# Seven block products on half tokens for the fourth group of the first feed-forward's second projection, beside the norms that follow it

## The reference, cut to what matters

```python
nm = rmsnorm(h, mlp_norm_g[l])
a = jnp.square(jax.nn.relu(jnp.einsum('bsd,df->bsf', nm, w_ff1[l])))    # 1024 -> 4096
h = h + jnp.einsum('bsf,fd->bsd', a, w_ff2[l])                          # 4096 -> 1024
...
x = rmsnorm(h, final_norm_g)                                            # end of layer one
...
xn = rms_norm(x, norm1_g)                                               # layer two
proj = xn @ w_in                                                        # q_sb first
```

## Time and profile before

| | us |
|---|---|
| median of 3 runs | 1363.39 (1362.97 to 1363.85) |
| the profiled execution, device time | 1364.07 |
| its span from first to last instruction | 1362.7 |
| PE busy | 1348.6 (99%) |
| DVE busy | 873.2 (64%) |
| ACT busy | 819.9 (60%) |
| POOL busy | 334.6 (25%) |

### The profile page before, as it was taken

One profiled execution on the slowest core, in us unless ns is written; L12 is line 12 of the kernel. 1 busy time (PEld: TensorE's weight loads), 2 busy tenths in 40 slices (PEclk: granted clock), 3 DMA queues, 4 the chain that ended last, 5 costly groups with the idle time before them and its releaser, 6 DMA issues.

```text
span 1362.7 us, 19539 instructions
## 1 busy us (share of the span) xinstructions
PE 1348.6 (99%) x7510; PEld 1135.7 (83%) x7510; DVE 873.2 (64%) x1548; ACT 819.9 (60%) x1235; POOL 334.6 (25%) x306
## 2 busy tenths in 40 slices
PE   9999999999999999999999999999999999999999
PEld 6977956789899898887777788888888898889889
DVE  6055466577576682357787779975437785568557
ACT  6575566753544545666577767775666645754553
POOL 0211101235343251111211121211113252315214
DMA  7976643925436137876654685668888536824733
GB/s 251 238 165 144 148 117 78 231 32 196 99 98 179 33 125 191 193 169 144 149 129 111 137 217 125 137 145 182 201 214 203 110 118 194 184 47 164 188 51 109
DMA packets 57969, 202.45 MB, mean 149 GB/s; under 512 B 6450, under 2 KB 7019, under 8 KB 57748
## 3 DMA queue, kind: packets, MB, share of 16 engines
q0 software_dynamic: 25632, 93.09, 36.4%
q1 hardware_dynamic: 31380, 106.24, 23.7%
q10 hardware_dynamic: 864, 1.87, 0.4%
HBM read 199.05 MB, written 2.12 MB: 148 GB/s over the span
## 4 chain that ended last, share of the span: by engine, by line
PE 77%; DVE 11%; ACT 8%; DMA 3%; issue 2%; SPq 0%; POOL 0%; DVEq 0%; ACTq 0%
PE bank L660 18%; PE bank L667 18%; PE bank L664 18%; PE bank L698 17%; DVE eb L1730 2%; PE bank L813 1%; ACT WL L1038 1%; ACT eb L1198 1%; ACT WH L1030 1%; ACT zs L1152 1%; PE bank L885 1%; DVE eb L1725 1%; DMA WL<-in_w_in 1%; DMA WL<-in_w_gu 1%; DMA RAW<-in_w_in 1%
## 5 line engine op out<-in xcount | busy, mean ns | idle before, releaser
L660 PE MATMUL bank<-NH,WH 128*128 128x512 f32 x1152 | 459.8, 400 | 0.3 <-ACT NH L1207 0.3
L664 PE MATMUL bank<-NL,WH 128*128 128x512 f32 x1152 | 448.1, 390 | 0.6 <-DVE NL L1470 0.5
L667 PE MATMUL bank<-NH,WL 128*128 128x512 f32 x1152 | 448.1, 390 | 0.6 <-DVE WL L1465 0.4
L660 PEld LDWEIGHTS bank<-NH,WH 128*128 128x128 f32 x1152 | 216.5, 188 | 60.2 <-issue 17.8
L667 PEld LDWEIGHTS bank<-NH,WL 128*128 128x128 f32 x1152 | 216.2, 188 | 47.5 <-DVE WL L1465 0.8
L664 PEld LDWEIGHTS bank<-NL,WH 128*128 128x128 f32 x1152 | 216.8, 188 | 44.7 <-DVE NL L1470 1.6
L1030 ACT ACTIVATE WH<-RAW 128x1024 fp32r<-128x1024 f32 (+3 forms) x148 | 152.1, 1032 | 74.4 <-PE bank L667 39.0
L698 PE MATMUL bank<-AH,WH 128*128 128x256 f32 x644 | 182.5, 283 | 0.3 <-DVE AL L2115 0.3
L698 PE MATMUL bank<-AL,WH 128*128 128x256 f32 x644 | 182.2, 283 | 0.0
L698 PE MATMUL bank<-AH,WL 128*128 128x256 f32 x644 | 182.2, 283 | 0.0
L1038 ACT ACTIVATE WL<-WH 128x1024 fp32r<-128x1024 f32 (+1 forms) x146 | 153.3, 1052 | 12.2 <-DMA WH<-in_w_in 9.9
(11 more groups left out here) (375 smaller groups left out, 2115.3 us busy)
## 6 DMA issues: line engine op xcount, KB each, us to landing
WL<-in_w_in POOLq DMA_DIRECT2D x58, 512.0 KB, 7.2
RAW<-in_w_gu SPq DMA_DIRECT2D x44, 512.0 KB, 5.1
WL<-in_w_gu POOLq DMA_DIRECT2D x34, 512.0 KB, 8.0
RAW<-in_w_ff SPq DMA_DIRECT2D x32, 512.0 KB, 4.6
WH<-in_w_in POOLq DMA_DIRECT2D x32, 512.0 KB, 7.1
RAW<-in_w_in SPq DMA_DIRECT2D x28, 512.0 KB, 6.4
quarters<-in_w_ff SPq DMA_DIRECT2D x24, 512.0 KB, 4.7
WL<-in_w_ff POOLq DMA_DIRECT2D x17, 512.0 KB, 6.5
```

What stands on the lines that cost most here:

```text
L660: e.matmul(o, a[0], a[1], start=(k == 0), stop=False)
L664: e.matmul(o, b[0], b[1], start=False, stop=False)
L667: mm = e.matmul(o, c[0], c[1], start=False, stop=(k == t.kt - 1))
```

## The change

The fourth group takes the form of the other three. `SEVENS` and `AHEAD` get an entry each (seven groups instead of six, so the indices of the gated feed-forward's move from 3 + g to 4 + g, and its first units from 12 and 13 to 16 and 17). `relu2(3)` now makes the pair sums, their rounded parts and rests in place of one high and one rest per tile. POOL makes quarter sums for four more units. The fourth group's weights are laid out in quarters. `to_h` for the group is replaced by `seven_out(3)`, whose finished rows carry the name `("h", "second", k)` for which the norm's generators wait. Nothing else of the norm is changed: its squares, sums, `NH` and `NL` rows keep their planned distance from the end of each row, and that end is now the plan's for a seven. The first five weight pieces of `qS` get their rest from DVE instead of a DMA, as after the other groups (`after`).

```diff
-SEVEN_GROUPS = 3
-SEVENS = [("f2", 0), ("f2", 1), ("f2", 2), ("dn", 0), ("dn", 1), ("dn", 2)]
-AHEAD = [("f1", 0), ("f1", 1), ("f1", 2), ("gu", 0), ("gu", 1), ("gu", 2)]
+SEVENS = [("f2", 0), ("f2", 1), ("f2", 2), ("f2", 3), ("dn", 0), ("dn", 1), ("dn", 2)]
+AHEAD = [("f1", 0), ("f1", 1), ("f1", 2), ("f1", 3), ("gu", 0), ("gu", 1), ("gu", 2)]
...
-            add(("f2", g), "w_ff2" if g < SEVEN_GROUPS else "w_ff2_last", 4 * g % (4 * SEVEN_GROUPS), 4 * g % (4 * SEVEN_GROUPS) + 4, 8, UC)
+            add(("f2", g), "w_ff2", 4 * g, 4 * g + 4, 8, UC)
...
-                    if g >= SEVEN_GROUPS:
-                        e.activation(AH1_last[:, t.i, :], f, ACT.Copy).then_inc(*act.sig(*hi(("f1", g), t.i)))
-                        return
...
                         if n == 4:
-                            at["h", ph, k] = at["h_part", u, 4]
+                            at["h", "second" if g == 3 else ph, k] = at["h_part", u, 4]
...
-                    at["h", ph, k1] = at["h_part", u, 6]
+                    at["h", "second" if g == 3 else ph, k1] = at["h_part", u, 6]
...
-                if g < SEVEN_GROUPS:
-                    streams += [*quarter_rests(g), seven_out(g)]
-                else:
-                    streams += [to_h(("f2", g), "second", lambda k, b=g - 1: ("h", ("f2", b), k))]
+                streams += [*quarter_rests(g), seven_out(g)]
```

More of the change, by code:

```diff
@@ L680, in seven @@
                 o = FB[seven_bank(s, bank)][:, 0:UC]
-                if n == 0 and s in (0, 1, 12, 13):
+                if n == 0 and s in (0, 1, 16, 17):
                     pe.wait_ge(*(f for f in fb["free"] if f))
@@ L700, in seven @@
                 mm.then_inc(*pe.sig("seven", t.u, n))
-                if s in (11, 23) and n == 6:
+                if s in (15, 27) and n == 6:
                     for i, key in enumerate((("h_part", plan.sevens[s - 1], 6), ("h_part", t.u, 6), ("h_part", t.u, 5), ("h_part", t.u, 4))):
@@ L1380, in rounded_part @@
                         lo_, hi_ = PART[part]
-                        e.activation(AH1[j][:, lo_:hi_], x, ACT.Copy).then_inc(*act.sig("pair_high", 3 + g, j, part))
+                        e.activation(AH1[j][:, lo_:hi_], x, ACT.Copy).then_inc(*act.sig("pair_high", 4 + g, j, part))
                     yield up_time(t, 1.0)
@@ L1766, in one_ @@
                     dve.wait_ge(("product", "tile", t.g), ("scale", "mlp"))
-                    if g >= SEVEN_GROUPS and t.i >= 3:
-                        dve.wait_ge(lo(("f1", g), t.i - 3))
-                    elif t.i >= 3 or g:
+                    if t.i >= 3 or g:
                         g0, i0 = (g, t.i - 3) if t.i >= 3 else (g - 1, t.i + 5)
@@ L1828, in seven_out @@
             def seven_out(g):
-                before, ph = ("mlp" if g == 0 else "ffn" if g == 3 else SEVENS[g - 1]), SEVENS[g]
+                before, ph = ("mlp" if g == 0 else "ffn" if g == 4 else SEVENS[g - 1]), SEVENS[g]
                 for t, t1 in zip(plan.stage[ph][::2], plan.stage[ph][1::2]):
@@ L2092, in gate @@
                         g0, k0 = (g, t.i // 2 - 3) if t.i >= 6 else (g - 1, t.i // 2 + 5)
-                        dve.wait_ge(*(("pair_low", 3 + g0, k0 // 2, part) for part in PART))
+                        dve.wait_ge(*(("pair_low", 4 + g0, k0 // 2, part) for part in PART))
                     e.tensor_tensor(x, bank_for(t), rs, ALU.mult).then_inc(*dve.sig("evac_v", t.g))
@@ L2113, in rest @@
                         lo_, hi_ = PART[part]
[L2114 removed]
+                        dve.wait_ge(("pair_high", 4 + g, j, part))
                         e.tensor_tensor(AL1[j][:, lo_:hi_], x, AH1[j][:, lo_:hi_].bitcast(F32),
[L2116 removed]
+                                        ALU.subtract).then_inc(*dve.sig("pair_low", 4 + g, j, part))
                     def difference(n, to, a, b, *waits):
                         dve.wait_ge(*waits)
[L2120 removed]
+                        e.tensor_tensor(to, a, b, ALU.subtract).then_inc(*dve.sig("pair_sum", 4 + g, j, n))
                     if k % 2 == 0:
                         yield up_time(t, 0.6)
[L2124 removed]
+                        back = [("pair_low", 4 + g, j - 1, "odd_sum") if j else ("pair_low", 3 + g, 3, "odd_sum")]
                         difference(0, T1, x[:, UC:], x[:, 0:UC], ("evac_v", t.g), *back)
@@ L2220, in moment @@
                         return seven_back(p) + (-0.24, 0.8, 2.37, 3.41, 4.45)[i] * plan.seventh(u)
-                    return due(f1[int(moments[i])], (8.0 if g > 2 and (n % 4, i) == (1, 4) else 0.9) + 7.6 * (moments[i] % 1))
+                    return due(f1[int(moments[i])], (8.0 if g > 3 and (n % 4, i) == (1, 4) else 0.9) + 7.6 * (moments[i] % 1))
                 def ahead(i):
```

29 lines of the change are left out of this document (9 added, 20 removed).

## The result

| | before | after |
|---|---|---|
| median of 5 runs | 1363.39 us (1362.97 to 1363.98) | 1383.24 us (1378.39 to 1384.74) |
| the profiled execution, device time | 1364.07 us | 1378.40 us |
| its span | 1362.7 us | 1377.1 us |
| predicted | | 1373.1 us, 1368.0 to 1377.5 |

The changed kernel is slower: ratio 1.0132, 95% interval 1.0117 to 1.0146. The direction was forecast, the time lies above the range. The runs of after spread over 6.4 us, those of before over 1.0. Two of the five stand at 1378.4 us and the profiled one is one of them, so the profile shows a mild case of what the median has.

A forecast was written before the change was run, and what follows sets the result against it. PE bounds the kernel before; in the changed stage DVE's queue makes PE wait. PE's saving -3.2, turns 1.7 + 7.4, group's end 1.0 and POOL surcharge 2.9 make +9.8 us: 1373.1 us, range 1368.0 to 1377.5.

The forecast's parts named there:

- PE's own work: Fourth group's matmuls: 336 of 256 columns replace 192 of 512, 40.3 us instead of 43.5, so 3.2 us less.
- The stage before it: In `("f1", 3)` DVE's pair sums and rests and POOL's quarter sums stay hidden behind PE's 43.6 us: no cost.
- The turns: From one unit's fourth product to the next's, DVE needs 13.8 us against PE's 10.08: waits 1.7, then twice 3.7 us.
- POOL's share: DVE's norm instructions beside POOL in the stage pay 0.32 us each, six per turn, one and a half turns: +2.9 us.
- More than PE's time: DVE in the fourth group's stage: 33.2 us plus the norm's 13.6, 46.8 us of instructions for 40.3 of PE.
- Faster: DVE keeps up: Rival, 3%: DVE's loop stays under 10.08 us, only PE's 3.2 us saving remains, 1360.2 us.
- The end of the group: In `qS`, PE's eighth block waits 1.0 us for DVE's last `NL` row.
- The clock at 1.00: PE's granted clock stays at 1.00 through the new waits, so no cost for a fall is in the sum.
- The waits drop TensorE's clock: Rival, 8%: the clock falls in PE's new waits, +2.9 us per wait, +6 to +9, about 1380 us.
- The sum: Whole kernel: -3.2 + 1.7 + 7.4 + 1.0 + 2.9 = +9.8 us, median 1373.1 us.

The follow-up runs named there:

- the run with the better order: Changed kernel with second square dropped, norm's rows and sums planned later, POOL's ten quarter sums on 4 columns: 1362.97 us, ratio 0.9985 to the kernel before.

## Why the prediction was right in direction and wrong in size

- **PE's own work, -3.2 us: right.** Starts 0.12 us apart, and 40.9 us for the stage once nothing waits.
- **The stage before it, nothing: right.** PE busy 44.2 of 44.2 us at 1.00.
- **The turns: 1.7, 3.7 and 3.7 us, and 2.9 of surcharge, 12.0 together; measured 4.4, 4.7 and 3.5, or 12.6.** (The usual 0.12 us between starts is taken off here.) The total is near, but partly by luck, as two errors cancel. The turns' own terms already held the weight rests at their slow mean, 0.65 us of POOL in each. Without it they should have come to 1.05, 3.05 and 3.05; the run without POOL's sums has 1.3, 3.5 and 3.5, 1.1 us more. Of that, 0.8 are the waits for ACT in the two full turns, 2.8 us each where the sum had 2.4.
- **POOL's share: 4.85 us in the sum (1.95 in the rests and 2.9 for the norm), 4.3 measured, but in other places.** The first turn paid 3.1 of it, the third nothing. The mechanism was right: of the norm's three instructions all pay beside POOL. The step "POOL prepares only the third and fourth unit within the stage, which covers about one and a half turns" at the mean surcharge of 0.32 per instruction failed as a way to place the cost. POOL's seven sums from 563.85 on run one behind the other, and the first turn's own instructions fall right among them. An instruction that meets one waits for its end, and next to POOL instructions in a row that is 1.0 to 1.1 us each time (1.78 and 1.75 against 0.74 and 0.69). The Trainium skill, SBUF — State Buffer, Who interferes with whom, calls the shared port pair an exclusive lock and says that VectorE instructions with two SBUF inputs contend for it; that the loser fully blocks it says there of VectorE's two-port modes. The trace agrees with a full block for two inputs as well: the sum over four columns took 1.22 us and ended with POOL's instruction. Such a block asks for counting meetings and not for a mean.
- **"More than PE's time", 46.8 us of DVE for 40.3: right as a sum, wrong as work.** The run without POOL's sums has DVE busy for 39.9 us of the same instructions, the run with the better order for 39.0 of 40.9. Some 6 us of the 46 are waits for POOL, which the profile shows as busy time; the 33.2 of the earlier trace rows held such waits too. That is why the rival "Faster: DVE keeps up" looked shut by instructions alone, while it needed POOL silent, another order and the second square gone.
- **The end of the group, 1.0 us: right,** 1.27 less the usual 0.23.
- **The clock at 1.00: the step that failed.** The sum put the clock's fall at nothing, and this is what took the time out of the range: with the gaps filled and the clock at 1.00 the kernel takes 1376.4 us, inside it. The rival "The waits drop TensorE's clock" had 8% and +2.9 per wait, about 1380 us. It happened, at 2.7 us in total in one profile and 7.0 in the other, 1.4 to 2.7 per fall and so at or under the rival's price; its chance was not right. The reason given against it, that no row shows a fall after a gap of this size, was no evidence: in the whole trace of the kernel before the longest distance between two starts of PE is 1.56 us, so there was no such gap to learn from. The price was worked out from PE's first matmuls as the slow level, where the column PEclk has 1.00 all the same; the slow level is shown by the runs here, 0.21 us against 0.12. The warning of the Trainium skill in TensorE: Matmul & The Clock Gate, Why this matters for your kernels, against idle gaps between bursts was the better guide, and the runs here agree with it.
- **The sum.** Predicted +9.8. The clock apart, the run with 24 extra matmuls has +12.3 in its profile and +12.7 in the median. Of the 2.5 us between +9.8 and +12.3, 1.5 lie in the stage: 0.6 in the three long waits, 0.5 in the short wait ahead of the third unit's third product, which had no term, and 0.4 in the four restarts, where the second start comes after 0.22 us instead of 0.12. Another 0.7 lie ahead of the stage and 0.3 behind it. The clock adds 6 to 7 in the median.

**Open.** Why the clock stays down for 6.8 us in one execution and for 3.4 in another, with the same long waits, the runs don't tell. And whether POOL's ten sums can be put where DVE doesn't meet them was not tried: it needs the quarters of the last two units earlier, and with them tiles that are in use.

## What to carry to other kernels

A stage in which one engine's work comes near the matmuls' time can turn a saving of matmuls into waits; count the instructions of that engine between two that PE waits for, and for each of them that reads two SBUF tiles ask which POOL instruction it will meet, at the price of what is left of that one. If a forecast has PE standing for longer than the trace has ever shown, here 3.7 us where 1.6 was the longest, it has no row on what the clock does then: put a fall into the sum, or into the range, and not only among the rivals. And where several things share one queue, expect each to help in part and none alone to be the cause. Against the changed kernel the norm's sums away were worth 10 us, POOL's sums away 8, the handover with ACT 4 (square left out) to 7 (own tile), each with its share of the clock, and both kinds of sums away 18. POOL's silence was still worth 8.5 us where handover and order were already mended.
